# Plain float32 projections in a decoder layer, and six weight slots in place of three

## The reference, cut to what matters

```python
h = rms_norm(x, norm_mix)
z = h @ w_in                      # 1024 x 4392: q, k, v of A; q and latent kv of B; index q, k, w; two gates
a = moba_attention(qa, ka, va, bias_a)                   # 8 heads of 64
b = dsa_attention(qb, kb, vb, iq, ik, iw, bias_b)        # 8 heads, 64 best keys chosen by relu(iq @ ik) * iw
m = (a @ w_oa) * sigmoid(ga) + (b @ w_ob) * sigmoid(gb)
x = x + m @ w_out
x = x + memory_cross_attention(rms_norm(x, norm_x), rms_norm(mem, mem_norm), wq_x, wk_x, wv_x, wo_x)
x = x + hier_moe(rms_norm(x, norm_moe), ...)             # 32 experts of 3 x 2 MB, 2 chosen for each token
return rms_norm(x, final_norm)
```

## Time and profile before

| | |
|---|---|
| time, median of 3 runs | 771.74 us (768.42 to 773.89) |
| span of the profiled execution | 771.6 us |
| PE busy | 576.0 us |
| DVE busy | 201.0 us |
| ACT busy | 154.8 us |
| from the start to the first matmul of the expert loop | 291.0 us |
| from there to the end | 480.6 us |

### The profile page before, as it was taken

How to read it: one execution, slowest core, us unless ns; L and a number is a source line. 1 busy time by engine, 2 the same in 40 slices (tenths; PEclk the granted TensorE clock), 3 DMA queues, 4 the chain that set the end, 5 groups by cost and what they waited for, 6 DMA issues and landing times.

```text
span 771.6 us, 9257 instructions
## 1 busy us (share of the span) xinstructions
PE 576.0 (75%) x3820; PEld 331.6 (43%) x3820; DVE 201.0 (26%) x362; ACT 154.8 (20%) x255; POOL 33.8 (4%) x34
## 2 busy tenths in 40 slices
PE   5989999999869799856665586674685667667554
PEld 4989998898769554311120131130131113013011
DVE  5468566357565441100000010010010000001001
ACT  5344445344434441000001000001000000100002
POOL 2000000011330100000000000000000000000001
PEclk9789999999989899998798886698879778669776
DMA  9895433523385686999999999999999999999991
GB/s 309 264 340 168 164 110 110 218 111 110 110 338 207 271 302 219 404 409 396 396 411 401 392 410 407 387 409 410 390 403 410 395 398 410 401 393 409 407 385 68
DMA packets 97358, 244.04 MB, mean 316 GB/s; under 512 B 9584, under 2 KB 18992, under 8 KB 97328
## 3 DMA queue, kind: packets, MB, share of 16 engines
q1 hardware_dynamic: 97328, 243.62, 83.6%
HBM read 242.53 MB, written 4.22 MB: 320 GB/s over the span
## 4 chain that ended last, share of the span: by engine, by line
SPq 48%; PE 32%; DMA 9%; DVE 4%; issue 3%; ACT 3%; POOL 0%; POOLq 0%; DVEq 0%; ACTq 0%
SPq L518 24%; SPq L520 15%; PE ps L643 13%; SPq L521 9%; PE ps L657 6%; DMA slots_late<-in_w 5%; DMA slots_own<-in_w 3%; PE ps L946 1%; PE ps L625 1%; PE ps L578 1%; PE ps L677 1%; PE ps L689 1%; DVE h_low L1401 1%; PE ps L974 1%; ACT xn L1002 1%
## 5 line engine op out<-in xcount | busy, mean ns | idle before, releaser
L946 PE MATMUL ps<-slots_late,ga 128*32 128x512 f32 x384 | 57.1, 725 | 35.6 <-DMA slots_late<-in_w 35.6
L422 DVE TENSOR_TENSOR w_low<-slots_own,w_high 128x2048 fp32r<-128x2048 f32 (+1 forms) x27 | 58.6, 2172 | 57.7 <-ACT w_high L1019 57.7
L643 PE MATMUL ps<-h_high,w_high 128*128 128x256 f32 x224 | 64.8, 289 | 0.0
L643 PE MATMUL ps<-h_high,w_low 128*128 128x256 f32 x224 | 63.6, 284 | 0.0
L643 PE MATMUL ps<-h_low,w_high 128*128 128x256 f32 x224 | 63.6, 284 | 0.0
L1019 ACT ACTIVATE w_high<-slots_own 128x2048 fp32r<-128x2048 f32 (+1 forms) x33 | 56.1, 1699 | 31.8 <-PE ps L657 17.7
L1533 DVE TENSOR_TENSOR bqT<-ps,bqT 128x512 f32<-128x512 f32 x8 | 5.5, 692 | 218.5 <-ACT bqT L1197 218.5
L964 PE MATMUL ps<-slots_own,vb 128*32 128x512 f32 x256 | 47.1, 869 | 17.6 <-DMA slots_own<-in_w 10.7
L946 PE MATMUL ps<-attn_data,ga 128*32 128x512 f32 x256 | 37.5, 722 | 21.0 <-DMA attn_data<-in_w 21.0
L946 PE MATMUL ps<-slots_own,ga 128*32 128x512 f32 x256 | 36.0, 689 | 21.8 <-DMA slots_own<-in_w 21.8
L643 PEld LDWEIGHTS ps<-h_high,w_high 128*128 128x128 f32 x224 | 43.4, 194 | 1.1 <-issue 1.1
(11 more groups left out here) (234 smaller groups left out, 791.9 us busy)
## 6 DMA issues: line engine op xcount, KB each, us to landing
slots_late<-in_w SPq DMA_DIRECT2D x24, 2048.0 KB, 23.8
attn_data<-in_w SPq DMA_DIRECT2D x16, 2048.0 KB, 21.5
slots_own<-in_w SPq DMA_DIRECT2D x16, 2048.0 KB, 21.2
slots_own<-in_w SPq DMA_DIRECT2D x32, 1024.0 KB, 16.3
slots_own<-in_w_in SPq DMA_DIRECT2D x8, 2048.0 KB, 9.1
slot_last<-in_w SPq DMA_DIRECT2D x8, 2048.0 KB, 24.2
attn_data<-in_w SPq DMA_DIRECT2D x16, 1024.0 KB, 14.1
slots_late<-in_w SPq DMA_DIRECT2D x16, 1024.0 KB, 14.4
```

The lines of the kernel that those rows point to most:

```text
L422: m = eng.tensor_tensor(low, src, high.bitcast(F32), ALU.subtract)
L643: m = pe.matmul(o[:, i * T:(i + 1) * T], w[:, k, c], x_[:, k, :], start=(k + j == 0), stop=(k == kk - 1 and j == 2))
L946: m = pe.matmul(ps[SLOTS * e:SLOTS * e + SLOTS, 4 + q % 2, :], xeT[:, k, SLOTS * e:SLOTS * e + SLOTS], w[:, e, kk, :], start=(k == 0), sto ...
```

## The change

All 34 jobs become plain float32 matmuls on the weights as they land and on one float32 tile of activations. The halves, their buffers, their semaphores and every instruction that made them go. The turned activations are scaled by ACT (blocks 0 and 2) and DVE (blocks 1 and 3). `ikw` loses its copied columns: the keys are computed four times, by matmuls with 32 columns of weights, each into another group of 32 PSUM partitions. The space that comes free makes the attention ring six slots long. The expert ring still has nine slots, taken in another order, and five of them can be filled as their last attention job is done.

```diff
-RING = 3
-MOE_SLOTS = [6, 7, 1, 2, 3, 4, 5, 8, 0]
+RING = 6
+MOE_SLOTS = [4, 5, 6, 7, 0, 1, 2, 8, 3]
...
             def fill(name, parts):
                 c = CHUNKS.index(name)
                 if c >= RING:
-                    chunk_done(LAST_JOB[CHUNKS[c - RING]])
+                    job_computed(sp, LAST_JOB[CHUNKS[c - RING]])
...
-            def split_columns(name, src, ready=None):
-                o = begin(name)
-                weights_split(pe, name)
...
-                        for j, (w, x_) in enumerate(((wh, src[0]), (wh, src[1]), (wl, src[0]))):
-                            m = pe.matmul(o[:, i * T:(i + 1) * T], w[:, k, c], x_[:, k, :],
-                                          start=(k + j == 0), stop=(k == kk - 1 and j == 2))
+            def projection(name, src, by_rows=False, ready=None):
+                weights_landed(pe, name)
+                w = weights(name)[1]
+                if by_rows:
+                    rows(name, w, src, range(TT), 0, 256, ready)
+                else:
+                    columns(name, w, src, ready)
...
+            for k in range(KD):
+                hT_ready(k)
+                for i in range(2):
+                    m = pe.matmul(o[:, i * T:(i + 1) * T], w[:, k, i * P:i * P + P], hT[:, k, :],
+                                  start=(i + k == 0), stop=(k == KD - 1), skip_group_check=True)
...
-            for k in range(KD):
-                for j, (w, x_) in enumerate(((wh, h_high), (wh, h_low), (wl, h_high))):
-                    pe.matmul(o[:, 0:T], w[:, k, 0:P], x_[:, k, :], start=(k + j == 0), stop=(k == KD - 1 and j == 2))
+            keys = w_ikw[:, :, 0:IDX_DIM]
+            for j in range(4):
                 for k in range(KD):
+                    pe.matmul(o[32 * j:32 * j + 32, 0:T], keys[:, k, :], hT[:, k, :],
+                              start=(k == 0), stop=(k == KD - 1))
             for t in range(TT):
                 for k in range(KD):
-                    for j, (w, x_) in enumerate(((wh, h_high), (wl, h_high), (wh, h_low))):
-                        m = pe.matmul(o[:, T + 8 * t:T + 8 * t + 8], x_[:, k, t * P:(t + 1) * P], w[:, k, P:IKW],
-                                      start=(k + j == 0), stop=(k == KD - 1 and j == 2))
+                    m = pe.matmul(o[:, T + 8 * t:T + 8 * t + 8], hT[:, k, t * P:(t + 1) * P], w_ikw[:, k, IDX_DIM:],
+                                  start=(k == 0), stop=(k == KD - 1))
...
-            pe.wait_ge(o_split, 8)
+            pe.wait_ge(o_copied, 8)
             for i in range(4):
-                split_columns(f"ob{i}", oB)
+                projection(f"ob{i}", oB)
...
-                split_rows(f"out{i}", h, merged_ready if i == 0 else None)
+                projection(f"out{i}", ga, by_rows=True, ready=merged_ready if i == 0 else None)
...
-                dve.tensor_tensor(pair(ga, i), pair(ga, i), pair(gb, i), ALU.add).then_inc(merge_added, 1)
-                after(f"ob{i}")
-                dve.wait_ge(merge_high, i + 1)
-                dve.tensor_tensor(pair(h_low, i), pair(ga, i), pair(h_high, i).bitcast(F32),
-                                  ALU.subtract).then_inc(merged_set, 1)
+                dve.tensor_tensor(pair(ga, i), pair(ga, i), pair(gb, i), ALU.add).then_inc(merged_set, 1)
```

More of the change, by code:

```diff
@@ L665, in _ @@
             m.then_inc(biasrow_done, 1)
+            weights_landed(pe, "iq")
+            w = weights("iq")[1]
             o = begin("iq")
-            wh, wl = part(w_high, "iq"), part(w_low, "iq")
-            for j, (w, x_) in enumerate(((wh, h_high), (wl, h_high), (wh, h_low))):
-                if j == 1:
-                    weights_split(pe, "iq")
-                for k in range(KD):
-                    if k % 2 == 0 and j != 1:
-                        pe.wait_ge((h_high_set, None, h_low_set)[j], k // 2 + 1)
-                    for i in range(2):
-                        m = pe.matmul(o[:, i * T:(i + 1) * T], w[:, k, i * P:i * P + P], x_[:, k, :],
-                                      start=(i + k + j == 0), stop=(k == KD - 1 and j == 2), skip_group_check=True)
@@ L704, in _ @@
             index_logits(0)
-            split_rows("ckv", h)
+            projection("ckv", hT, by_rows=True)
             pe.wait_ge(relu_set, 1)
@@ L1044, in _ @@
             copy_job("iq", iqT[:].rearrange("p a b -> p (a b)"))
-            after("iq")
-            after("ikw")
             act.wait_ge(idx_done, 1)
@@ L1054, in _ @@
                 square(o[:, t * RANK:(t + 1) * RANK], 4, t, junk[:, 4 + t, :], csq_done)
-            after("ckv")
             act.wait_ge(idx_done, 2)
@@ L1064, in _ @@
             evacuates(m, "ckv")
-            for b in range(4):
-                split_turned(1, b, 1, tT_high)
+            for b in (0, 2):
+                scale_turned(1, b, 1, tT)
             o = job_computed(act, "ckvT")
@@ L1134, in _ @@
                     copy_o(n - 1)
-                if names:
-                    after(names[1])
                 if n < 8:
                     exps(n)
-            for i in range(4):
-                after(f"ob{i}")
-                act.wait_ge(merge_added, i + 1)
-                act.activation(pair(h_high, i), pair(ga, i), ACT.Copy).then_inc(merge_high, 1)
             act.wait_ge(small_in, 16 * 7)
-            for i in range(4):
-                after(f"out{i}")
-                if i:
-                    split_turned(2, i - 1, 2, tT_high)
-            split_turned(2, 3, 2, tT_high)
+            for b in (0, 2):
+                scale_turned(2, b, 2, tT)
+            act.wait_ge(resid_set, 4)
             square(x_sb[:, 0, :], 2, 0, xn[:, 0, :], squares[0])
@@ L1303, in _ @@
                         dve.wait_ge(idx_added, 1)
-                        after("ckv")
             wait_marked()
-            for b in range(4):
-                split_turned(1, b, 1, tT_high, tT_low)
+            for b in (1, 3):
+                scale_turned(1, b, 1, tT)
             segs = (slice(0, P), slice(P, 3 * P))
@@ L1385, in _ @@
                     logits(n)
-                if n >= 1:
-                    split_o(n - 1)
-                if names:
-                    after(names[1])
                 if n < 8:
@@ L1598, in _ @@
             finish_gates(ga, "ga")
[L1599 to L1602 removed]
+            finish_gates(gb, "gb")
             of_d_model(2)
```

207 lines of the change are left out of this document (50 added, 157 removed).

## The result

| | before | after |
|---|---|---|
| time, median of 4 runs each | 771.38 us (768.42 to 773.89) | 787.02 us (785.5 to 787.26) |
| ratio | | 1.0211 (95%: 1.0169 to 1.0253) |
| span of the profiled execution | 771.6 us | 785.4 us |
| first matmul of the expert loop | 291.0 us | 306.2 us |
| from there to the end | 480.6 us | 479.2 us |

The account below looks back on a forecast made before the run. PE was taken to bound the kernel until 291 us, then the expert-weight stream for 480.6 us. Stage terms 6.2 - 1.1 + 6.8 + 6.8 + 3.9 - 3.5 + 1.1 = +20.2 gave 792 us; own range 787 to 797, 0.8 range 782 to 803.

Parts of the forecast that it names:

- The cost of a job: Each full projection job on PE: 32 records of 0.215 us, 6.9 us, 1.14 us more than before.
- The keys: Key columns in the first stage: four groups overlapping by three waiting records, 52 steps, 11.2 us.
- iq: First job of the kernel: first 3 us at the low clock, 8.4 us against 7.3 before.
- Index logits and ckv: Stage after the gate columns: ckv 8.3 us, ACT's weight split gone before the relu; 12.4 us, -1.1.
- aq to av: Stage before the scores: six jobs with PE full, 6 x 1.14 = +6.8 us.
- Steps 4 to 8, ob and out: Later attention: more PE work less removed waits, +3.9 us in steps 4 to 8, -3.5 in ob and out.
- qx to the router: Last stage before the expert part: one longer job, +1.1 us, with the cross attention chain unchanged.
- SP and the expert part: Weight fills and expert loop: no chunk late before, same expert code and stream; 0 each, expert spread +-2.5 us.
- The low clock under 32 columns: Rival for key and gate columns: narrow matmuls let the clock fall, 11 us more, 803 us; chance 0.15.
- four groups at once: Rival for the keys: all groups run together in 3.5 to 4 us, 7.4 us less, 784 us; chance 0.12.
- the late start of the stream: Rival at the expert loop: stream starts on fewer full slots after a late xo3, +5 us; chance 0.05.
- The cheaper plain record: Rival in all jobs: plain float32 record under 0.215 us, change not slower, equal at 0.194; chance 0.04.

Follow-up runs that it names:

- keys_run1: Changed kernel with the key matmuls going round the four column groups, one matmul (two records) to a group in turn; 780.07 us, ratio 1.016.
- after: The changed kernel itself, all jobs plain float32, in its first measurement against the kernel before; 787.02 us, ratio 1.0211.
- after_again: The changed kernel, unmodified, run a second time on another chip beside a three-slot version; 786.7 us, ratio 1.023 to the kernel before.
- experiment 5: Changed kernel with two unread copies put back on ACT ahead of the second relu, restoring the wait; 790.21 us in one run.
- plain_splits_kept: Kernel before with all jobs but iq and ikw as plain float32 matmuls, all halves still made and waited for; 795.94 us, ratio 1.034.

## Why the prediction was right

The forecast was 792 us, the measurement 787.02, inside the range and inside the forecast's own range at its lower bound (787). The first expert matmul was told for 311 us and came at 306.2. By the steps of the prediction:

- **The cost of a job.** 0.215 us a record and 6.9 us a job were forecast from the latent job; 0.216 and 6.91 were found in every such job at the full clock. Steps 1 to 3 came out at +6.86 for +6.8.
- **The rule of four passes.** The prediction took it as four times the 0.120 us of one float32r record and got 0.48 us. That was my reading of it, not the rule: 0.431 us at 2.4 GHz is 1034 cycles for 256 columns, four to a column, and the 0.120 us record is 288 cycles, 1.1 to a column. The Trainium skill (FP8 and Floating Point Precision, TensorE Precision Notes) and the trace agree if a pass is counted as 256 cycles. The "25 x 0.8" beside it is also too few: 24 full and 8 half jobs are 28 full ones, 22 us. Nothing in the forecast rests on either.
- **The keys.** 11.2 us forecast, 11.43 found, and the mechanism (a change of group once three records are left) held in four orders of issue. The Trainium skill's up to four times the speed for 32 columns (TensorEngine Tiling (Array Packing), Theoretical Speedup) is nearly reached in keys_run1 (3.59 us for the 13.8 that 64 steps would be), but not by a loop that finishes one group before the next. The Trainium skill's rule of strict program order (TensorE: Matmul & The Clock Gate, Part 3, The mechanism) doesn't hold in this trace between column groups, as the second group's first record starts before the first group's last ones. The prediction priced that rule at 13.8 us; starts in program order still let each group's last record run beside the next group's first, which makes 61 steps, 13.2 us.
- **iq.** 8.4 us forecast, 7.1 found. The step that failed is that the first 3 us would again be at the low level. When the clock first rises is a matter of the single launch: 12.2 to 18.8 us in the profiles of this study, of which two of one kernel (after, after_again) have 14.0 and 12.5. It is worth up to 2 us, and I can't say what sets it. That it rose before iq in this profile and not in the one of before is luck, not the change.
- **Index logits and ckv.** 12.4 us forecast, 12.2 found. The end of the squares, 0.9 us after ckv, was told as what is late next; the second relu starts at 47.99 us, when they and the second index logits have both just ended.
- **aq to av.** +6.8 forecast, +4.2 found: the mis-sized term. The jobs themselves were right (27.63 + 13.81 us for six of them); what the sum left out is that the shorter wait before them keeps the clock up (experiment 5). I had read the low clock at 45 us as a thing of the place, not of the wait. The turns took 2.1 us less and the first records behind them 0.6.
- **Steps 4 to 8, ob and out.** +3.9 and -3.5 forecast, +4.05 and -3.8 found. plain_splits_kept shows in these stages what the removed waits were worth, with the low clock behind them: 3.5 and 7.2 us.
- **qx to the router.** +1.1 forecast, +0.2 found: qx took its 6.92, but the low clock that both kernels have in the cross attention ended (at 283.6 us) in the middle of the 16 records of L739, which took 2.61 us for 3.67. This is chance too. In after_again, the same kernel, they took 3.67 us and the stage, between first matmuls, is 1.1 us longer than before:

```profile
281.35 3.67 PE ps L739 x16
```

- **SP and the expert part.** 0 and 0; no PE wait for a DMA with three slots or with six, and between the kernels 4.0 and 1.2 us in the two comparisons, with spreads of some 4 us each, which leaves this term open; 1.4 us in the expert part, inside its forecast spread of 2.5.
- **The rivals.** The low clock under 32 columns (803) and four groups at once (784) both fell, and so did the late start of the stream (the expert part is no longer than before). The second is true of another order of issue, and then gives what was said of it: 7 us. The cheaper plain record fell with the 0.216.

All misses over 0.25 us go one way, 6.4 us together against the span of 785.4 and 5 us against the median. All but the expert part's 1.4 and 0.3 in ob and out have their place in the clock, and they are of two kinds. 2.7 us (aq to av) come from the change: where it takes a wait away, the work behind the wait gets cheaper too, and the prediction should have had it. Some 2.3 us in iq and L739 come from when the clock happened to rise in the two profiled executions. A sum of durations taken from a profile carries with it the clock that this profile had. That the median ended just inside the forecast's own range is in part luck.

## What to carry to other kernels

Work taken from an engine counts for what PE waited for it, not for its busy time: 153 us of DVE, ACT and POOL work were worth about 14 us of the end, in the places that the waits name, while 1.15 us more for each full job was paid in full. So a cheap matmul form that needs preparation belongs where PE is full and a dear one without it where PE would wait for the preparation; choosing by job gave 0.988, choosing one form for all gave 1.021 (6.6 us of that difference are iq and ikw). When narrow matmuls go to several column groups, go round the groups every few matmuls: the same instructions took 3.6 us and not 11.4.

## What the hardware showed that I had not expected

- Between groups of 32 output columns the records overlap as long as no more than three of one group have to wait: 3.59, 3.66, 8.10 and 11.43 us for 64 records in runs of 2, 4, 8 and 16. Four records to a run cost nothing against two, eight double the time. Records of the second group start ahead of records that come before them in the program.
- A wait of 2.9 us in front of 16 transposes brought the granted clock to 0.5 for 3.4 us, one of 3.2 us for 3.4 us in one profile and 6.8 us in two, and one of 1.6 us in the same place left it at 1.0 in eight profiles.
- A kernel that pauses PE less often keeps its clock: 10.2 us at the low level between 20 us and the expert loop, in both profiles of the changed kernel, where the kernel before had 34, of which 10.2 began under the gate columns and not in a pause.
- When the clock first rose differed by up to 6.6 us between profiles (12.2 to 18.8 us) and by 1.5 us between two of one kernel.
